# The first mixer's sixteen gate columns on TensorE: from 24 products of 256 columns each to 8 products of 512 and 8 of 256

## What is computed

```
hx = modulate(rmsnorm(x, norm1_g), ...)             # 256 x 1024
hc = modulate(rmsnorm(ctx, norm1_g), ...)           # 256 x 1024
ux = hx @ w_in ; uc = hc @ w_in                     # w_in: 1024 x 5120
ox = hgrn_bidir(...)                                # gated scan over the tokens, both directions
y_a = fourier_mix(ux[fnet columns]) @ w_a
y_b = hgrn_readout(ux, ox) @ w_b
g_a = sigmoid(ux[GA columns])                       # 8 blocks of 128 columns
g_b = sigmoid(ux[GB columns])                       # 8 blocks of 128 columns
y   = (g_a * y_a + g_b * y_b) @ w_out
```

## Time and profile of the kernel before

| what | value |
|---|---|
| median of three runs | 850.33 us (848.76 to 852.48) |
| the profiled execution, its own time | 849.34 us |
| its span | 847.3 us, 14837 instructions |
| matmuls (PE) | 835.3 us busy, 5858 |
| weight loads (PEld) | 766.1 us busy, 5858 |
| VectorE (DVE) | 577.3 us busy, 1214 |
| ScalarE (ACT) | 476.9 us busy, 793 |
| GpSimd (POOL) | 353.2 us busy, 173 |
| TensorE's mean granted clock | 0.999 of full speed |

### The profile page before, as it was taken

One profiled execution on the slowest core, in us unless ns is written; L12 is line 12 of the kernel. 1 busy time (PEld: TensorE's weight loads), 2 busy tenths in 40 slices (PEclk: granted clock), 3 DMA queues, 4 the chain that ended last, 5 costly groups with the idle time before them and its releaser, 6 DMA issues.

```text
span 847.3 us, 14837 instructions
## 1 busy us (share of the span) xinstructions
PE 835.3 (99%) x5858; PEld 766.1 (90%) x5858; DVE 577.3 (68%) x1214; ACT 476.9 (56%) x793; POOL 353.2 (42%) x173
## 2 busy tenths in 40 slices
PE   9999999999999999999999999999999999999997
PEld 4578999998899999999999988999999888888886
DVE  4789879886467896767677879686448445444445
ACT  7353345443766655555555864555447666666665
POOL 0000000001751598888887300200000788888883
PEclk9999999999999999999999999999999999999999
DMA  9998556654275556555555546364535556566651
GB/s 350 367 384 272 202 208 214 206 168 140 73 253 182 175 182 194 178 193 176 184 189 176 162 150 197 101 194 127 179 100 174 174 177 198 183 195 191 198 178 73
DMA packets 44742, 161.37 MB, mean 190 GB/s; under 512 B 5105, under 2 KB 5377, under 8 KB 43522
## 3 DMA queue, kind: packets, MB, share of 16 engines
q1 hardware_dynamic: 44384, 159.38, 58.0%
q10 hardware_dynamic: 290, 1.05, 0.3%
HBM read 159.37 MB, written 1.05 MB: 189 GB/s over the span
## 4 chain that ended last, share of the span: by engine, by line
PE 87%; DVE 6%; ACT 3%; DMA 2%; issue 1%; POOL 1%; ACTq 0%; DVEq 0%; POOLq 0%
PE bank L667 13%; PE bank L672 13%; PE bank L670 12%; PE bank L1104 9%; PE bank L1110 5%; PE bank L1193 2%; PE bank L1195 2%; PE bank L1197 2%; PE bank L1143 2%; PE bank L1141 2%; PE bank L1145 2%; DVE wlo L526 2%; PE bank L1003 2%; PE bank L769 1%; PE bank L771 1%; PE bank L775 1%
## 5 line engine op out<-in xcount | busy, mean ns | idle before, releaser
L526 POOL TENSOR_TENSOR wlo<-raw,whi 128x1024 fp32r<-128x1024 f32 (+1 forms) x147 | 334.8, 2300 | 407.2 <-ACT whi L1375 407.0
L1375 ACT ACTIVATE whi<-raw 128x1024 fp32r<-128x1024 f32 (+1 forms) x253 | 258.6, 1026 | 66.7 <-PE bank L672 22.6
L1824 DVE SCALAR_TENSOR_TENSOR accs<-bank,vec,accs 128x189 f32<-128x189 f32 (+4 forms) x440 | 161.1, 433 | 71.2 <-ACT accs L1687 71.2
L526 DVE TENSOR_TENSOR wlo<-raw,whi 128x1024 fp32r<-128x1024 f32 x106 | 129.0, 1229 | 29.1 <-ACT whi L1375 28.4
L667 PE MATMUL bank<-h,whi 128*128 128x256 f32 x504 | 143.7, 286 | 0.0
L672 PE MATMUL bank<-h,whi 128*128 128x256 f32 x504 | 142.3, 283 | 0.0
L670 PE MATMUL bank<-h,wlo 128*128 128x256 f32 x496 | 140.5, 283 | 0.7 <-DVE wlo L526 0.7
L667 PEld LDWEIGHTS bank<-h,whi 128*128 128x128 f32 x504 | 96.6, 192 | 0.7 <-issue 0.3
L672 PEld LDWEIGHTS bank<-h,whi 128*128 128x128 f32 x504 | 96.7, 192 | 0.0
L670 PEld LDWEIGHTS bank<-h,wlo 128*128 128x128 f32 x496 | 95.1, 192 | 1.1 <-DVE wlo L526 1.0
L1104 PE MATMUL bank<-h,whi 128*128 128x512 f32 x352 | 88.4, 392 | 0.5 <-DVE gl L1821 0.4
(11 more groups left out here) (362 smaller groups left out, 1851.0 us busy)
## 6 DMA issues: line engine op xcount, KB each, us to landing
raw<-in_up SPq DMA_DIRECT2D x88, 512.0 KB, 3.5
raw<-in_w_in SPq DMA_DIRECT2D x45, 512.0 KB, 4.5
raw<-in_down SPq DMA_DIRECT2D x44, 512.0 KB, 3.5
ada_sc<-in_ada SPq DMA_DIRECT2D x8, 1024.0 KB, 19.9
ada_kT<-in_adaT SPq DMA_DIRECT2D x16, 512.0 KB, 4.7
raw<-in_w_out SPq DMA_DIRECT2D x16, 512.0 KB, 4.5
raw<-in_w_in_t SPq DMA_DIRECT2D x12, 512.0 KB, 4.5
ada_sc<-in_adaT SPq DMA_DIRECT2D x8, 512.0 KB, 7.7
```

The lines of the kernel that those rows point to most:

```text
L526: return e.tensor_tensor(wlo[:, j % HL, 0:k], raw[:, j % RAW, 0:k], whi[:, j % HL, 0:k].bitcast(F32), ALU.subtract)
L1375: e.activation(whi[:, j % HL, 0:(k1 - k0) * 128], raw[:, j % RAW, 0:(k1 - k0) * 128], ACT.Copy).then_inc(S.hi.up(j))
L1824: return e.scalar_tensor_tensor(out=out, in0=a, scalar=s, in1=b, op0=o1, op1=o2)
```

## The change

`hch` and `hcl` become the two halves of one tile `hc2`, [128, 2, 8, 512], at the same addresses. A gate column is made by `gate_wide`: for each k one product of whi with both halves of the operand (high into the bank's first 256 columns, low into its second), then eight of wlo with the high half. ScalarE copies the second half of the bank to `gab` (signal `gpart`), VectorE adds the first half to it (`gate_sum`, signal `gsum`), and ScalarE makes the Sigmoid in place, three columns later (the last three after the last filler). The bank is free again with `gsum` instead of `gab`. In VectorE's order the add stands in `beside`, behind `los` of its filler and ahead of `ada_step`.

```diff
-        put("hch", Z, [128, 8, 512], F32R)
-        put("hcl", Z + 16, [128, 8, 512], F32R)
+        put("hc2", Z, [128, 2, 8, 512], F32R)
+        M["hch"], M["hcl"] = M["hc2"][:, 0, :, :], M["hc2"][:, 1, :, :]
...
+            gsum = signal("gsum", range(16))
+            gpart = signal("gpart", range(16))
...
+                elif kind == "g":
+                    slot, free = lin_ring.take((kind, n), S.Gs, n)
+                    lin("w_in", IN_G + n, banks[slot][:, 0:L], hc_x, free)
                 else:
-                    slot, free = lin_ring.take((kind, n), *{"g": (S.Gs, n), "gate": (S.gab, n)}[kind])
-                    lin("w_in", (IN_G if kind == "g" else IN_GA) + n, banks[slot][:, 0:L], hc_x, free)
+                    slot, free = lin_ring.take((kind, n), S.gsum, n)
+                    gate_wide(n, banks[slot], free)
+
+            def gate_wide(n, ps, free):
+
+                c = ch("w_in", IN_GA + n)
+                wh, wl = weights(c)
+                w.wait_ge(*free)
+                w.wait_ge(S.hi, c)
+                for k in range(KT):
+                    e.matmul(ps.rearrange("p (v t) -> p v t", v=2), wh[:, k, :], M["hc2"][:, :, k, 0:L], start=k == 0,
+                             stop=False, skip_group_check=True)
+                w.wait_ge(*lo(c))
+                for k in range(KT):
+                    t = e.matmul(ps[:, 0:L], wl[:, k, :], xh(k)[:, 0:L], start=False, stop=k == KT - 1,
+                                 skip_group_check=True)
+                t.then_inc(S.chunk.up(c))
...
+            def gate(n):
+                w.wait_ge(S.gsum, n)
+                e.activation(M["gab"][:, n, :], M["gab"][:, n, :], ACT.Sigmoid).then_inc(S.gab.up(n))
...
-                    e.activation(M["gab"][:, n, :], ps[:, 0:L], ACT.Sigmoid).then_inc(S.gab.up(n))
+                    e.activation(M["gab"][:, n, :], ps[:, L:2 * L], ACT.Copy).then_inc(S.gpart.up(n))
                 if (kind, n) in second:
                     near(second[kind, n])
+                if kind == "gate" and n >= 3:
+                    gate(n - 3)
+            for n in range(13, 16):
+                gate(n)
...
+            def gate_sum(n):
+                ps = lin_bank(("gate", n))
+                w.wait_ge(S.gpart, n)
+                tt(M["gab"][:, n, :], ps[:, 0:L], M["gab"][:, n, :], ALU.add).then_inc(S.gsum.up(n))
...
                     if kind == "g":
                         gate_value(n)
+                    if kind == "gate":
+                        gate_sum(n)
                 ada_step()
```

## The result

The changed kernel takes 854.51 us (median of 7 executions, 854.20 to 855.35), the kernel before beside it 848.90 (median of 7). The ratio is 1.0062, 95% interval 1.0053 to 1.0071: 0.62% slower, some 5.3 us. That lies in the stated range (850.8 to 855.5), but beyond the 0.5% within which I had put it with a chance of 0.81, and 1.8 us above the number of my own case. The shift is missed by more than that, 2.4 us forecast and some 5.3 measured: the three runs that I had of the kernel before had a median 1.4 us above that of the seven. Counted as a shift from them the range ended at +5.2, so the number lies in it only because its starting point was 1.4 us too high. The profiled execution has 854.45 us, its span went from 847.3 to 852.4.

What follows compares the result with a forecast made beforehand. TensorE's queue was taken as the bound (835.3 us of matmul in a span of 847.3). Terms -1.4 + 0 + 0.2 + 3.6 = +2.4 us took 849.34 to 851.7, or 852.7 against the median; range 850.8 to 855.5.

Steps and rivals of the forecast that it cites:

- my own case: Whole kernel: the four parts sum to +2.4 us, median 852.7, within what a measurement can tell; chance 0.72.
- Part 1: Gate columns on TensorE: wide products save 0.087 us a column, 1.4 us over 16 columns.
- Rival C: Gate columns: wide products save nothing over two operand pieces; +3.8 us, median 854.1, chance 0.05.
- Part 2: Inside the levels: added Copy, add and moved Sigmoid cost nothing, covered by VectorE's idle time; levels 10.16 us.
- Part 3: Far scores, last level: VectorE's modulation row waits for GpSimd's low half, so TensorE waits 0.2 us; bounds 0 and 1.6.
- rival A: Last level: both GpSimd low halves get in ahead of VectorE, 1.6 us instead of 0.2; +3.8, median 854.1, chance 0.12.
- P + 1.35 against P + 1.45 and P + 5.9: From level start P: GpSimd's low half due at 1.35, VectorE's modulation row at 1.45, GpSimd's next low half at 5.9 us.
- Part 4: Last three columns: far copies behind column 15's add leave TensorE idle 3.3 us, product of Q 0.3 more; together 3.6.
- The 0.3 for the product of Q: Just after the heads' first products: TensorE waits another 0.3 us because the last product of Q is late.
- Rival B: Gap ahead of the heads: TensorE's clock falls to 1.2 GHz; +5.0 us, median 855.4, chance 0.08.
- The price, 2.6 us: Loss if the clock falls in the gap ahead of the heads: half speed for 5.3 us loses 2.6.
- The 5.3 us themselves: Kernel start: six passes of 512 columns took 5.29 us, taken as the length of half speed after a clock fall.

Runs made afterwards that it cites:

- run 4: Changed kernel with VectorE's add of column 15 behind the far copies and GpSimd held until the update of level 6: 848.45 us against 849.53, ratio 0.9988.
- run 1: Changed kernel with VectorE's add of column 15 moved behind the far copies and the last product of Q: 849.27 us against 849.53, ratio 1.0001.
- run 6: Kernel before, with only a VectorE wait added for column 15's Sigmoid ahead of the seventh level's modulation row: 852.99 to 855.58 us, ratio 1.0058.
- run 8: Changed kernel with three dummy products filling TensorE's gap between column 15 and the heads: 854.28 us.
- run 9: Changed kernel unaltered, measured again beside other runs on one chip: 854.30 us, ratio 1.0058 to the kernel before.
- run 2: Changed kernel with GpSimd held (the hold) until the update of level 6, before its first low half of w_a: 853.91 us, ratio 1.0055.
- run 5: Changed kernel with the modulation row ahead of the add of column 15 instead of behind it: 853.43 us, ratio 1.0049.
- run 10: Changed kernel with GpSimd held until the update of level 6 and three dummy products in the gap ahead of the heads: 851.67 us, ratio 1.0027.
- run 7: Kernel before with VectorE's added wait for column 15, and three dummy products in the gap: 852.76 us against 849.05, ratio 1.0040.

## Why the prediction was right or wrong

**Part 1, the columns: right.** 0.082 us a column, 1.3 in all, where I had 0.087 and 1.4; run 4 has them alone. Rival C is out.

**Part 2, the levels: right.** 10.17 us for 10.16, VectorE 0.64 us idle ahead of a level's last low half in level 4 and 0.67 in level 5 (I had 0.4 to 0.7), no wait of TensorE in any middle level.

**Part 3, the far scores: mechanism right, size off.** I took 0.2 us for a first collision with GpSimd and left a second one, up to 1.6 in all, to rival A, because it needed 0.1 us of timing twice. Both collisions came, so rival A came true, at 1.1 us and not 1.6: they cost VectorE 1.0 (2.26 for 1.28) and 1.1 (2.37 for 1.28), where I had 1.2 and 1.4. They came again in every profile of the changed kernel without the hold. The margin was small but not a matter of luck: the order of two engines' starts follows from the same rows in each execution, and I had worked out P + 1.35 against P + 1.45 and P + 5.9 against the product after it. Having both, I should have followed them through. With the slower passes behind the wait the term was 1.4 us, not 0.2.

**Part 4, the last columns: right on the gap, wrong on what follows it.** A gap of 3.4 us (3.3 expected), for the reason given, shown by run 1 from one side and by run 6 from the other. SP and ScalarE cost nothing. The 0.3 for the product of Q shows only where the clock stays up (runs 6 and 8).

**Rival B was no rival but a part of the likeliest case, and that is the step that failed.** I took from one row that the clock falls some 3.9 us after TensorE stops and concluded that a gap of 3.3 us is safe. The runs show falls 3.5 and 3.9 us after the stop (changed kernel, here and in run 9), 2.3 us (run 2) and 3.9 us (run 5, with TensorE at work again for 1.7), and none at all after a gap of 3.1 us in the profile of run 6. One row gives one of the possible delays, not the least. The page of the Trainium skill that I weighed against it (TensorE: Matmul & The Clock Gate, Why this matters for your kernels), with its warning of idle gaps between bursts of matmuls, was the better guide here. The trace agrees with it in the changed kernel, where the clock fell after a gap of 3.4 us, and not in the profile of run 6. What decides when the clock falls stays open. The price, 2.6 us, was too high: 1.7, since the low stretch lasted 3.4 us and not 5.3, and 1.4 net, since it covered the 0.3 us wait for Q. The 5.3 us themselves were a weak source: over the kernel's first microseconds the granted clock reads 1.00, so that no row shows those passes to have run at the low level.

So the sum should have been -1.3 for the columns, +1.4 for the far scores, +3.4 for the gap, +0.2 for the first pair after it (0.67 for 0.43, run 6) and +1.7 for the clock: +5.4, and the stage is 5.39 us longer. Why the first passes after a wait take more is not settled.

The number lay in the range by luck. The range was wide enough for A or for B alone; both came, each cheaper than I had priced it, and the start was 1.4 us too high. My own case, with 0.72, did not come true.

## What to carry to other kernels

When an add or a copy is put into an engine's hand-written order, list what stands behind it in that queue at the last place where it occurs, not only in the steady state: the levels hid fifteen adds, and the sixteenth held back the heads. On a kernel whose matmul engine never waits, price a new gap of 2 to 3 us with the low clock behind it. The columns' 1.3 us can be had here only if the other engines' order is moved with them, as in run 4.

## What the runs showed of the hardware that I had not expected

The clock can fall while TensorE is already at work again: in run 5 the gap ended at 201.78 and the products slowed at 203.5. And nearly the same gap can cost nothing or much: a gap of 3.1 us with no fall (run 6), 3.4 us with 3.4 us of low clock (changed kernel), 3.4 us with 6.8 (run 2). Executions of one kernel differ by 2.6 to 3.1 us (runs 6 and 2), but those of the changed kernel lie within 0.4 in run 9 and within 1.2 in the first seven.

A low clock can come elsewhere too: in the profiles of runs 8 and 10 it was low for some 3.4 us inside the kernel's first 20 us, and their scans began 1.2 and 1.6 us later than the changed kernel's. The kernel before spreads over 4.4 us beside run 7; where it loses them, no trace here shows.
